# A hybrid diffusion step on one core: delta-branch preparation under the in-projection, attention and mod products in another order

## The reference

```python
proj = h @ w_in
a_qkv, b_qkv, b_z, b_ab = jnp.split(proj, ...)          # attention A | delta B | gate z | decays
b_qkv = jax.nn.silu(_dwconv_centred(b_qkv, conv_w))      # three taps along the tokens
qb, kb = _l2norm(qb), _l2norm(kb)
g = -jnp.exp(a_log) * jax.nn.softplus(ab[:, :, 0] + dt_bias)
beta = jax.nn.sigmoid(ab[:, :, 1])
gc = jnp.cumsum(g, axis=-1)
decay = jnp.where(lower, jnp.exp(jnp.where(lower, diff, 0.0)), 0.0)      # diff = gc_i - gc_j
lmat = jnp.where(strict, jnp.einsum('nbhid,nbhjd->nbhij', kb, k) * decay, 0.0)
tinv = lax.linalg.triangular_solve(eye + lmat, ...)      # the solve
...
p = jax.nn.softmax(s, axis=-1).astype(v.dtype)           # mixer A; the sample group also reads the cache
return jnp.einsum('bhqk,bkhd->bqhd', p, v)
...
x = x + gt1 * mix                                        # mix = concat(A, gated B) @ w_out
x = x + gt2 * _channel_mixer(h, l, ffn_gate, ffn_up, ffn_down, w_router, moe_gate, moe_up, moe_down)
```

## Time and profile before

| | |
|---|---|
| median of three runs | 1449.45 us (1448.61 to 1450.89) |
| span of the profiled execution, first to last instruction | 1446.3 us |
| PE busy over the span | 1368.2 us, 95% |
| DVE, ACT, POOL busy | 328.7, 304.1, 95.5 us |
| DMA | 500.24 MB, mean 346 GB/s |

### The profile page before, as it was taken

How to read it: one execution, slowest core, us unless ns; L and a number is a source line. 1 busy time by engine, 2 the same in 40 slices (tenths; PEclk the granted TensorE clock), 3 DMA queues, 4 the chain that set the end, 5 groups by cost and what they waited for, 6 DMA issues and landing times.

```text
span 1446.3 us, 28143 instructions
## 1 busy us (share of the span) xinstructions
PE 1368.2 (95%) x12676; PEld 723.2 (50%) x12676; DVE 328.7 (23%) x415; ACT 304.1 (21%) x402; POOL 95.5 (7%) x175
## 2 busy tenths in 40 slices
PE   4998889989999998999999999999999999999976
PEld 1995587668888876343334333333333343343322
DVE  1444653745544446000000000000000000000005
ACT  2444543353334334010000010010000010010002
POOL 5100132420000001000000000000000000000012
PEclk9899999989999999999999999999999999999999
DMA  8846817989555549999999999999999999999995
GB/s 337 295 175 252 314 62 273 361 313 391 192 185 192 177 143 401 412 411 425 421 423 425 403 423 409 401 418 425 405 416 425 402 416 424 406 414 424 421 421 203
DMA packets 125186, 500.24 MB, mean 346 GB/s; under 512 B 10716, under 2 KB 14632, under 8 KB 103568
## 3 DMA queue, kind: packets, MB, share of 16 engines
q1 hardware_dynamic: 110464, 471.98, 82.0%
q10 hardware_dynamic: 12208, 18.12, 3.4%
q0 software_dynamic: 2400, 8.42, 1.5%
HBM read 478.81 MB, written 19.69 MB: 345 GB/s over the span
## 4 chain that ended last, share of the span: by engine, by line
PE 74%; DMA 6%; SPq 3%; DVE 2%; ACT 1%; issue 1%; ACTq 0%; DVEq 0%
PE ps L2129 33%; PE ps L2177 12%; PE ps L409 5%; PE ps L410 5%; PE ps L411 5%; DMA raw<-in_moe_down 4%; SPq L534 3%; PE ps L2172 3%; PE ps L1659 3%; DMA ring_b<-in_moe_down 2%; PE ps L1673 1%; PE ps L1884 1%; PE ps L1875 1%; PE ps L1862 1%; PE ps L2050 0%
## 5 line engine op out<-in xcount | busy, mean ns | idle before, releaser
L2129 PE MATMUL ps<-raw,hTf 128*32 128x512 f32 (+1 forms) x2128 | 209.7, 545 | 3.3 <-DMA raw<-in_moe_up 3.2
L2129 PE MATMUL ps<-ring_a,hTf 128*32 128x512 f32 (+1 forms) x2096 | 203.0, 538 | 2.1 <-ACT hTf L1093 1.1
L1611 DVE TENSOR_TENSOR hm<-gate_bc,ps 128x384 f32<-128x384 f32 (+1 forms) x30 | 18.1, 607 | 711.7 <-PE ps L2129 710.9
L372 DVE TENSOR_TENSOR w_lo<-raw,w_hi 128x2048 fp32r<-128x2048 f32 x60 | 138.6, 2323 | 148.2 <-ACT w_hi L368 148.2
L2129 PE MATMUL ps<-ring_b,hTf 128*32 128x384 f32 (+1 forms) x1408 | 139.2, 540 | 3.5 <-DMA ring_b<-in_moe_up 2.2
L368 ACT ACTIVATE w_hi<-raw 128x2048 fp32r<-128x2048 f32 x60 | 114.0, 1914 | 117.4 <-PE ps L411 110.4
L2129 PEld LDWEIGHTS ps<-raw,hTf 128*32 128x32 f32 x2128 | 68.2, 110 | 130.3 <-issue 124.5
L2129 PEld LDWEIGHTS ps<-ring_a,hTf 128*32 128x32 f32 x2096 | 67.9, 110 | 122.2 <-issue 117.8
L409 PE MATMUL ps<-w_hi,hTh 128*128 128x512 f32 x272 | 106.6, 392 | 1.5 <-DVE w_lo L372 1.5
L410 PE MATMUL ps<-w_hi,hTl 128*128 128x512 f32 x272 | 105.9, 389 | 0.0
L411 PE MATMUL ps<-w_lo,hTh 128*128 128x512 f32 x272 | 105.9, 389 | 0.0
(11 more groups left out here) (374 smaller groups left out, 1494.1 us busy)
## 6 DMA issues: line engine op xcount, KB each, us to landing
raw<-in_w_mod SPq DMA_DIRECT2D x48, 1024.0 KB, 6.8
raw<-in_moe_down SPq DMA_DIRECT2D x21, 2048.0 KB, 24.3
ring_a<-in_moe_down SPq DMA_DIRECT2D x21, 2048.0 KB, 25.4
raw<-in_moe_up SPq DMA_DIRECT2D x14, 2048.0 KB, 23.8
ring_b<-in_moe_down SPq DMA_DIRECT2D x14, 2048.0 KB, 24.8
ring_a<-in_moe_gate SPq DMA_DIRECT2D x13, 2048.0 KB, 20.9
raw<-in_moe_gate SPq DMA_DIRECT2D x11, 2048.0 KB, 23.4
ring_a<-in_moe_up SPq DMA_DIRECT2D x10, 2048.0 KB, 18.5
```

What stands on the lines that cost most here:

```text
L372: nc.vector.tensor_tensor(w_lo[:, w % SPLIT], raw[:, slot % RAW], w_hi[:, w % SPLIT].bitcast(F32), ALU.subtract).then_inc(s["lo_ready"], 1)
L2129: last = MM(ps[TOK * j:TOK * j + TOK, part % 4, 0:w], hTf1[:, kt, q * P + TOK * g:q * P + TOK * g + TOK], wt[:, kt % 2, j, :], start=kt == ...
```

## The change

Nothing is computed differently. What moves, by engine:

- ACT and DVE take the decays, the conv, the spread's differences and exponentials, the SiLUs and the squares into the in-projection, one chunk at a time, between the splits. The conv's buffers become `X` and `XT`.
- PE takes the cumulated sums behind the second chunk, the two spreads behind the third and fourth, and the sums of squares with the key transposes behind the sixth.
- `w_out`'s first two units are loaded ahead of mod groups 1 and 2 and split under the last chunk; before, they were split later, DVE's part inside the solve.
- Behind the in-projection PE now runs: broadcast of the lengths, scores, the first key products, mod group 1, the transposes of the probabilities, two units of group 2, attention output, value transposes, second key products, transposes of L, the rest of group 2. The key products of the two token groups go through bank 6, one behind the other. DVE masks both before it evicts the attention output.
- On ACT the row copies of groups 1 and 2 have new places: ahead of the softmax exponentials, and ahead of the solve's first saves.
- The first state product (line 1842) moves from ahead of the solve to behind its level 0.
- POOL's broadcast of the decays no longer waits for the last eviction, and its half of the diagonal goes ahead of the scaling of z.

```diff
-ORDER = (mods(0) + splits(0, WOUT) + mods(1) + mods(2) + splits(WOUT, WOUT + 2) + mods(3) + mods(4) + splits(WOUT + 2, MOE)
+ORDER = (mods(0) + splits(0, WOUT + 2) + mods(1) + mods(2) + mods(3) + mods(4) + splits(WOUT + 2, MOE)
...
-            for i in range(MOD_KT, 3 * MOD_KT):
-                mod_load(i)
             for i in range(2):
                 wout_load(i)
-            for i in range(3 * MOD_KT, 5 * MOD_KT):
+            for i in range(MOD_KT, 5 * MOD_KT):
                 mod_load(i)
             for i in range(2, 4):
...
-            pool.wait_ge(s["proj_saved"], 7)
+            pool.wait_ge(s["len_inverse"], 1)
+            nc.gpsimd.tensor_tensor(XT[:, 0:8], rep(ident[:, :], 1, 8), rep(sm[:, 17, 0:8], 2, P), ALU.mult)\
+                .then_inc(s["len_diag"], 1)
...
-            for i in range(len(WIN_ORDER)):
-                unit_hi(act, 2 * i)
-                if i:
-                    copy_proj(i - 1)
-                unit_hi(act, 2 * i + 1)
-            copy_proj(len(WIN_ORDER) - 1)
...
+            unit_hi(act, 0)
+            unit_hi(act, 1)
+            unit_hi(act, 2)
+            softplus_in()
+            copy_proj(0)
+            unit_hi(act, 3)
+            conv_middle(0)
+            unit_hi(act, 4)
+            copy_proj(1)
+            unit_hi(act, 5)
+            conv_middle(1)
+            unit_hi(act, 6)
+            copy_proj(2)
+            unit_hi(act, 7)
+            conv_middle(2)
...
+            unit_hi(act, 8)
+            copy_proj(3)
+            unit_hi(act, 9)
+            decay_exp(0)
+            unit_hi(act, 10)
+            copy_proj(4)
+            unit_hi(act, 11)
+            decay_exp(1)
+            for j in range(3):
+                conv_silu(j)
+            act.wait_ge(s["conv_done"], 3)
+            nc.scalar.activation(X.rearrange("p (a c) n -> p a (c n)", c=2), b_ch[:, 0:8], ACT.Square).then_inc(s["sq_ready"], 1)
+            unit_hi(act, 12)
+            copy_proj(5)
+            unit_hi(act, 13)
+            unit_hi(act, 14)
+            act.wait_ge(s["k_turned"], 1)
+            nc.scalar.activation(kcT[:, :, :], ps[:, 2].rearrange("p (a n) -> p a n", n=P), ACT.Copy).then_inc(s["k_saved"], 1)
+            nc.scalar.activation(kc[:, :], ps[:, 3], ACT.Copy).then_inc(s["k_saved"], 1)
+            act.wait_ge(s["ss_turned"], 1)
+            nc.scalar.activation(sm[:, 16], ps[:, 6, 0:16], ACT.Sqrt, bias=eps[:, 0:1]).then_inc(s["rq_ready"], 1)
+            unit_hi(act, 15)
+            act.wait_ge(s["k_saved"], 2)
+            act.wait_ge(s["proj_saved"], 6)
+            act.dma_start(new_k[0, 0].rearrange("t h d -> t (h d)"), kc[:, :]).then_inc(s["kv_stored"], 16)
+            act.dma_start(new_v[0, 0].rearrange("t h d -> t (h d)"), vA[:, 0]).then_inc(s["kv_stored"], 16)
+            copy_proj(6)
+            act.wait_ge(s["proj_saved"], 7)
+            nc.scalar.activation(z[:, :, :], z[:, :, :], ACT.Silu).then_inc(s["silu_z"], 1)
...
+            preload(ACT.Exp, 3)
+            copy_rows(1, 7)
             for i in range(3):
                 act.wait_ge(s["p_in"], i + 1)
                 nc.scalar.activation(PR[i], PR[i], ACT.Exp).then_inc(s["p_exp"], 1)
-            copy_rows(2, 7)
...
-            for i in range(WOUT, WOUT + 2):
-                unit_hi(act, i)
...
+            copy_rows(2, 7)
...
+            unit_lo(dve, 0)
+            unit_lo(dve, 1)
+            gates_in()
+            unit_lo(dve, 2)
+            gates_out()
+            unit_lo(dve, 3)
+            conv_taps(0)
+            unit_lo(dve, 4)
+            unit_lo(dve, 5)
+            dve.wait_ge(s["gc_turned"], 1)
...
+            conv_taps(1)
+            unit_lo(dve, 6)
+            unit_lo(dve, 7)
+            conv_taps(2)
+            decay_in(0)
+            unit_lo(dve, 8)
+            unit_lo(dve, 9)
+            decay_in(1)
+            for i in range(10, WOUT + 1):
+                unit_lo(dve, i)
+            dve.wait_ge(s["rq_ready"], 1)
...
+            unit_lo(dve, WOUT + 1)
+            dve.wait_ge(s["len_turned"], 1)
+            nc.vector.scalar_tensor_tensor(qv, qv, DK ** -0.5, inv[:, 0:8], ALU.mult, ALU.mult).then_inc(s["qn_ready"], 1)
+            VT(kv, kv, inv[:, 8:16], ALU.mult).then_inc(s["kn_ready"], 1)
...
-            save_cols(2, 7)
-            scales(1, 3)
+            save_cols(1, 7)
...
+            dve.wait_ge(s["L_beta"], 2)
+            for b in range(NB):
+                dve.wait_ge(s["qk_turned"], b + 1)
+                for d in range(2):
+                    cut = slice(8 * b + 4 * d, 8 * b + 4 * d + 4)
+                    last = VT(CTa[:, cut], bank(6), X[:, cut], ALU.mult)
+                last.then_inc(s["L_masked"], 1)
             for b in range(NB):
                 dve.wait_ge(s["o_turned"], b + 1)
...
-            update_level(0)
-            unit_lo(dve, WOUT)
-            update_level(1)
-            unit_lo(dve, WOUT + 1)
-            update_level(2)
+            save_cols(2, 7)
+            scales(1, 3)
+            for l in range(3):
+                update_level(l)
...
+                if i == 1:
+                    cumulate()
+                if i in (2, 3):
+                    spread_rows(i - 2)
+                if i == 5:
+                    lengths_and_keys()
...
+            pe.wait_ge(s["len_diag"], 2)
+            pe.wait_ge(s["proj_saved"], 6)
+            for i in range(4):
+                last = MM(ps[:, 4 + i, :], ones[:, :], XT[:, 4 * i:4 * i + 4].rearrange("p a n -> p (a n)"), start=True, stop=True)
+            last.then_inc(s["len_turned"], 1)
+            pe.wait_ge(s["proj_saved"], 7)
             scores(0, kTA, 0, 0, False)
-            turn_cols(1, 7)
+            pe.wait_ge(s["k_saved"], 2)
             scores(1, kTA, P, 2, True)
-            pe.wait_ge(s["k_saved"], 2)
+            pe.wait_ge(s["qn_ready"], 1)
             scores(1, kcT, 0, 4, False)
...
+            pe.wait_ge(s["kn_ready"], 1)
+            key_products(0)
+            for i in range(MOD_KT, 2 * MOD_KT):
                 mod_product(i, 7)
             for i in range(3):
+                pe.wait_ge(s["p_in"], 3)
+                pe.wait_ge(s["p_exp"], i + 1)
                 for h in range(8):
                     last = turn(ps[:, 2 * i + h // 4, (h % 4) * P:(h % 4 + 1) * P], PR[i][:, h])
                 last.then_inc(s["p_turned"], 1)
-            turn_cols(2, 7)
+            turn_cols(1, 7)
+            pe.wait_ge(s["mod_cols_saved"], 2)
+            for i in range(2 * MOD_KT, 2 * MOD_KT + 2):
+                mod_product(i, 7)
+            pe.wait_ge(s["pT_saved"], 3)
...
+            pe.wait_ge(s["L_masked"], 1)
+            key_products(1)
             for b in range(NB):
                 pe.wait_ge(s["L_masked"], b + 1)
                 if b:
...
+                if b == 0:
+                    mod_product(2 * MOD_KT + 2, 7)
+            for h in range(H_B):
+                last = turn(ps[:, 6, h * P:h * P + P], tile(1, h, 0))
+            last.then_inc(s["ktok_turned"], 1)
+            for i in range(2 * MOD_KT + 3, 3 * MOD_KT):
+                mod_product(i, 7)
...
+            turn_cols(2, 7)
+            pe.wait_ge(s["oa_ready"], 2)
...
+                if l == 0:
+                    pe.wait_ge(s["ktok_saved"], 3)
+                    pe.wait_ge(s["mod_cols_saved"], 3)
+                    for d in range(2):
+                        for h in range(H_B):
+                            last = MM(ps[:, 6 + d, h * P:h * P + P], tile(1, h, 1), s0[:, d, h], start=True, stop=True)
+                    last.then_inc(s["ks_turned"], 1)
```

More of the change, by code:

```diff
@@ new lines, in conv_middle, with conv_silu @@
+            def conv_middle(j):
+                act.wait_ge(s["proj_saved"], j + 1)
+                for t in range(4 * j, 4 * j + 4):
+                    nc.scalar.activation(conv_tmp(t), b_ch[:, t], ACT.Identity, scale=conv_cols[:, 1, t:t + 1])\
+                        .then_inc(s["conv_mid"], 1)
+            def conv_silu(j):
+                act.wait_ge(s["conv_sum"], 8 * j + 8)
+                nc.scalar.activation(b_ch[:, 4 * j:4 * j + 4], (X[:, 8 * j:8 * j + 8] if j < 2 else XT[:, 0:8])
+                                     .rearrange("p (a c) n -> p a (c n)", c=2), ACT.Silu).then_inc(s["conv_done"], 1)
@@ new lines, in decay_exp @@
+            def decay_exp(b):
+                act.wait_ge(s["diff_ready"], b + 1)
+                nc.scalar.activation(decay[:, 8 * b:8 * b + 8], decay[:, 8 * b:8 * b + 8], ACT.Exp, scale=-1.0)\
+                    .then_inc(s["decay_ready"], 1)
+            unit_hi(act, 0)
[7 more added lines that the diff above has]
+            copy_proj(1)
@@ L1828, in _ @@
             last.then_inc(s["v_turned"], 1)
-            for h in range(H_B):
-                last = turn(ps[:, 6, h * P:h * P + P], tile(1, h, 0))
-            last.then_inc(s["ktok_turned"], 1)
+            pe.wait_ge(s["L_masked"], 1)
+            key_products(1)
             for b in range(NB):
@@ L1838, in _ @@
```

(7 more changed lines are left out.)

220 lines of the change are left out of this document (83 added, 137 removed).

## The result

The changed kernel takes 1436.87 us (median of 4, 1435.34 to 1442.14) where the kernel before takes 1450.17 (1448.61 to 1453.11): ratio 0.9905, 95% interval 0.9884 to 0.9927. A second comparison, with 5 runs beside 17, gave 0.9908 (0.9891 to 0.9924). It is 13.3 us faster; the forecast was 3.6. Its profiled execution spans 1435.6 us, 10.7 less than the profile of before.

A forecast was written before the change was run, and what follows sets the result against it. Bound: PE never pausing in the in-projection, then a relay of PE, DVE and ACT, none full. Sum 49.0 − 67.9 + 13.35 + 1.95 = −3.6 us, median 1445.9; forecast range 1444 to 1448, chance 0.45.

The forecast's parts named there:

- PE's additions under the in-projection: In-projection: cumulated sums 1.4, two spreads 4.1, sums of squares 4.1 and key transposes 0.9 cost PE 10.5 us.
- The clock behind the sums: In-projection behind the one-column sums of squares: the clock falls to half, costing 2.85 us, ends 0 and 3.4.
- rival A1: In-projection: the clock holds under the one-column products, 2.85 us less, median 1443.0; chance 0.20.
- Behind the in-projection: From the in-projection's end to the solve's first product: 49.0 us against 67.9, exponentials waiting behind the row copy.
- rival A2: Behind the in-projection: clock also holds through DMA waits, 0.9 less at the last mod unit, 2.8 at transposes; 1439.3; chance 0.07.
- The state products: In the solve: products of keys with the state, moved behind level 0, add 1.95 us, ends 0 and 3.0.
- The splits: In-projection: weight splits on ACT and DVE stay on time, first chunk tightest with margin 0.3; 0 us, other end 1.5.
- Rival B: Behind the in-projection: half clock lasts through the attention output, work then takes twice 7.8 us; 1453.7; chance 0.11.
- C: In-projection: taps and exponentials delay low parts, a microsecond in each of three chunks; 1448.9, no visible difference; chance 0.17.

The follow-up runs named there:

- the run with late units: Changed kernel with the softmax exponentials before group 1's row copy, its last two units behind the probability transposes, group 2's first two units later; 1435.57 us, ratio 0.9891.
- the last kernel: Changed kernel with exponentials first, group 1's last two units behind the transposes, rows turned between attention-output halves, sums of squares 128 columns wide; 1435.50 us, ratio 0.9888.

## Why the prediction was right and wrong

The direction, the place and the order of events held; the sizes of the terms did not. The step that failed is the pricing: durations were carried over from rows of before that lay in the half clock of the earlier trace rows (the cumulated sums, the end of the one-column products, the first scores, the end of mod group 1), and the new order was charged for further half clock, as if it belonged to the work. The forecast for chunk 0 to the out-projection was −3.6, and the first two profiles have −13.3. The 9.7 between them, term by term:

- **PE's additions under the in-projection: 10.5 forecast, 8.5 measured.** The cumulated sums cost 0.66, not 1.4 (the second chunk takes 12.18 against 11.52), a spread 1.78, not 2.05 (13.30 against 11.52), sums and keys 4.3, not 5.0. The row of the cumulated sums, 138.83 to 140.22, lies wholly in the half clock of 136.5 to 143.0, and the last microsecond of the one-column products, 157.21 to 161.33, in that of 160.3 to 167.1. The spread's row counts the end of its last product, beside which the next work already runs here.
- **The clock behind the sums: 2.85 forecast, 0 in the profile, 1.6 in six profiles of seven.** The step was right in kind, and rival A1, which the profile alone would seem to confirm, is not what usually happens. The size failed because the row of before was taken for the price: there the clock stayed low for 6.8 us, here it was low for 3.70 us at a mean of 0.55, which is 1.7 lost. The Trainium skill, page "TensorE: Matmul & The Clock Gate", Part 1, has it that activity releases the throttle; taken as PE being busy, the runs here speak against it, since PE was busy for 4.40 of 4.40 us ahead of the fall, and for all 16.60 us of the long one. (That PE had no idle time ahead of the fall of before, as the prediction has it, is true only from 155.35 on; the profiles of after settle it.)
- **Behind the in-projection: 49.0 forecast, 45.2 measured (45.2 to 46.2 in three profiles).** The order of events is the predicted one, and the late copy of the rows held the exponentials as it said. Counted from z's copy, the mod units began 9.4 behind it, not 10.4: the first scores took 1.09, where the prediction took 2.0 from a row in the half clock, 140.22. The eight units took 9.7, not 11.0: 0.9 because the clock held through the last of them (1.07 us for 1.94), the rest because PE stood 2.17 for the two loads, not 2.73. The 24 transposes took 4.0, not 5.6, since the clock was back before they ended. From the attention output on, each step is as long as forecast. Of the 3.8 gained here, some 2.5 are of the two kinds that rival A2 named (0.9 and 2.8); but the clock did fall, one step later than the forecast had it.
- **The state products: +1.95 forecast, +0.65 measured.** With the pauses taken off it is about +2.0, the size of the forecast; but leaving the products out gave back only 0.7 to 1.4, so it is not shown that they account for all of it. The pauses were 1.4 shorter in this profile. They vary by 2.4 among runs of the same code, so this part is chance.
- **The splits:** forecast on time, and they were. But the tight place was not the first chunk, where the prediction looked. At the last chunk the low part is ready at 124.20 and PE wants it at 125.18, and only because sums and keys (from 120.86) stand ahead of it; take the sums away and PE waits 2.44 for it, take both away and it waits 3.33. On ACT, the high part that DVE needs first stands behind the SiLUs and the squares which the change moved there (lines 890 and 928):

```profile
115.18 2.95 ACT L890 ACTIVATE b_ch<-T 128x1024 f32<-128x1024 f32 x3
118.16 1.92 ACT L928 ACTIVATE T<-b_ch 128x2048 f32<-128x2048 f32 x1
119.99 1.89 ACT L372 ACTIVATE w_hi<-raw 128x2048 fp32r<-128x2048 f32 x1
```

```profile
121.91 2.29 DVE L376 TENSOR_TENSOR w_lo<-raw,w_hi 128x2048 fp32r<-128x2048 f32 x1 [6.67 <-ACT w_hi L372]
```

The prediction followed this list to the squares and no further. So the 4.3 us of PE's work there cost only about 1 beyond a wait that ACT's moved work would have made anyway. This changes no term of the sum, but it is why taking that work out again won so little under the in-projection.

Rival B (the half clock lasts through the attention output) didn't occur in any profile, nor did C. Of the 13.3 to 13.9 us between the medians, the spans of the first two profiles have 10.7, and three profiles of after with two of before give 10.7 for chunk 0 to the out-projection (196.6 against 207.4). The other 3 us or so stay open: the kernel before ran between 1446.18 and 1458.59 in the long comparison, and both its profiles (spans 1446.3 and 1446.4, the second with a time of 1448.15) lie near the lower end, so what its longer runs lose is in no trace here.

## What to carry to other kernels

A price read from a stretch at half clock, or between other engines' waits, is not the price of that work elsewhere: take it from a row at full clock and carry the clock as a term of its own, with both ends. Before charging an engine for work that is moved under a stage, look at whether the same move makes that engine wait there, because the work then fills the wait. And when a pause is removed that stood for a load, ask which load comes next: here one arrived every 2.4 us, and the pause moved to the end of the next group, whose last unit landed no earlier.

## What the runs showed of the hardware

- Sixteen one-column products in a row (3.5 us, PE busy throughout) were followed by a granted clock of 0.50 in six of seven profiles, and with forty-eight it stood at 0.50 for 16.6 us, PE busy throughout; the same sixteen, 128 columns wide, took as long and were followed by none in two. What the chip counts is not shown by this.
- Where the clock falls differs from run to run of the same kernel: a fall of 6.5 us at 136.5 in one profile of before is absent in the other, where m1 comes 2.5 us earlier behind z's copy.
- PE pauses in the solve for up to 2.1 us with no releaser in the profile, at places that change from run to run (0 to 3.5 us in sum). All 25 of these pauses end 1.25 to 1.50 us behind a packet on the core's instruction queue; that PE waits for its own instructions there fits this, and was not tested.
- A load of 1 MB that is queued behind another lands 2.4 us after it: PE's starts that waited for two such loads are 2.44 to 2.45 apart in the changed kernel, in the run with late units and in the last kernel.
